# Splitting the modulation products of a two-layer diffusion backbone over two column groups of TensorE, with one buffer for each row made during routing

## The chip, the cores and the metric

The kernel runs on one core of a Trainium2 chip. The metric is the device time of one execution in microseconds (us); a lower time is better. TensorE (PE in the profile) does the matrix products, VectorE (DVE) and ScalarE (ACT) the elementwise work, GpSimd (POOL) and SyncE (SP) issue the DMAs here. "Record" below means one matmul instruction as the trace lists it; an f32 product of 128 rows by 512 columns appears as two records.

## What is computed

A backbone of two layers over 256 latent tokens and 256 context tokens, model width 1024. Cut to what matters:

```python
for l in range(DEPTH):                                   # DEPTH = 2
    mod   = silu(c)     @ w_mod[l] + b_mod[l]            # (1, 6144), for latent tokens
    mod_c = silu(c_ctx) @ w_mod[l] + b_mod[l]            # (6144,),  for context tokens
    sh1, sc1, g1, sh2, sc2, g2 = split(mod, 6)           # and the same of mod_c
    h = rmsnorm(x, norm1[l]) * (1 + sc1) + sh1
    q, k, v of three branches, gates = split(h @ w_in[l])
    x = x + g1 * merge(global attention, window attention, neighbourhood attention)
    h = rmsnorm(x, norm2[l]) * (1 + sc2) + sh2
    x = x + g2 * moe(h)        # 16 experts of width 512, top 2 inside the best group of 4
return rmsnorm(x, final_norm)
```

The context tokens go through layer 0 in the same way and serve as keys and values in both. The modulation vectors are two rows (one for `c`, one for `c_ctx`) of 6144 values per layer. All products are f32.

## The kernel before

**Weights.** All weights but the small ones pass through a ring of six SBUF slots of 2 MB (`ring`, `WR[slot]`). SyncE issues the loads in one fixed order (`plan_units`, `load`, L422 for `w_mod` and `w_in`, L438 for experts). A load into a slot waits until the last product that read the slot is done (`releases`); the first twelve loads also keep three in flight (`AHEAD = 3`: load i waits for modulation i-3).

**Modulation.** The 6144 columns of a layer are made in twelve pieces of 512, numbered i = 0 to 23 over both layers, j = 0 to 11 within one. `modulation(i)` on TensorE (L1369) multiplies `cT` (128 x 2 per step) by the 2 MB slot in KD = 8 steps, 16 records, into rows 0 and 1 of one PSUM bank, `MOD_BANK[i]`; a bank that was used before is waited for by `mod_row`. `mod_rows(i)` on VectorE adds the bias (L920; L916 and L917 for the two scale parts, which are also multiplied with the norm weight) and writes a row buffer `mrow` of 2 x 512. `store_mod` on GpSimd (L518) stores the buffer to DRAM (`mod_d`), from where GpSimd later loads it back broadcast over 128 partitions (`load_modb` L528, `load_gout` L549).

**When they run.** Twelve pieces of layer 0 come first. Between them stand the four transposes of the first normed rows (`transpose_h`, L1348), and behind them the projections of layer 0 (L1418), of which the first needs the `kvab` weights. Of layer 1, piece 12 comes right behind the router product (L1502), before TensorE waits for VectorE's selection (`sel_ready`) and computes positions (L1535, L1538); pieces 13 to 19 follow it and then the first expert's transposes (`transpose_rows(0)`). Pieces 20 to 23 follow the last expert of layer 0.

**Routing.** VectorE computes for every token its two experts and slots, with `mod_rows(12)` in the middle and `mod_rows(13..19)` behind. As soon as the slots are known (`slot_ready`), GpSimd scatters the 512 normed tokens twice to DRAM (`hs_d`, eight indirect DMAs, L591), waits for all of them, loads the rows of experts 0 and 1 (`load_rows`, L600), and only then stores the modulation rows 13 to 19 one after the other, loads the modulation of layer 1 (L528) and the rows of expert 2.

**Row buffers.** In layer 0 four buffers rotate, in layer 1 two: before it writes row i, VectorE waits for the store of row i-4, or i-2 in layer 1 (`mod_store`).

**Experts.** Three 2 MB weights per expert (gate L1584, up L1591, down L1614). An expert with at most 64 rows takes another form, two products in the upper and lower 64 output partitions at the same time (gate and up L1598, down L1620).

## Time and profile before

| | |
|---|---|
| median of 3 runs | 1875.71 us (1874.19 to 1879.04) |
| the profiled execution | 1875.32 us |
| its span | 1873.7 us |
| TensorE busy | 1696.4 us, 91% |
| VectorE busy | 463.4 us, 25% |
| ScalarE busy | 339.6 us, 18% |
| moved by DMA | 396.74 MB, mean 212 GB/s |
| matmuls of the modulation, L1369 | 384 records, 170.6 us |

The page divides the span into 40 slices of 46.8 us and gives each engine's busy share in tenths. The timeline gives merged runs of equal instructions in order of time: start, length, engine, line, operation, count, and in brackets the idle time before and what ended it. The stretches view gives busy time, granted TensorE clock (1.00 is 2.4 GHz, 0.50 is 1.2 GHz), DMA share and GB/s of a stretch; a DMA share of about 1.04 is the highest that lasts.

### The profile page before, as it was taken

What the parts mean: (1) busy time and instruction counts of PE and PEld (TensorE: products, weight loads), DVE (VectorE), ACT (ScalarE), POOL (GpSimd) and SP (SyncE); (2) the same over time, 40 slices, a digit from 0 to 9 for tenths busy, and PEclk for the clock granted to TensorE, in tenths of its full rate; (3) what the DMA queues carried; (4) which work ended last, traced back from release to release, by engine and by line L of the source; (5) the groups of instructions that cost most, each with busy time, mean ns of one, the idle gap of its engine ahead of it and who ended that gap; (6) DMA issues with size and microseconds to landing.
All of it is one profiled execution on the core that took longest, in us unless ns stands there. A gap on an engine that the chain in (4) does not pass through costs nothing. (4 is left out here: it accounts for less than half of the span.)

```text
span 1873.7 us, 15998 instructions
## 1 busy us (share of the span) xinstructions
PE 1696.4 (91%) x6163; PEld 758.0 (40%) x6163; DVE 463.4 (25%) x1206; ACT 339.6 (18%) x759; POOL 132.2 (7%) x219
## 2 busy tenths in 40 slices
PE   7999998889999999999999989998799949987871
PEld 1244445554444445244444324445544424432220
DVE  0324016760011123210110145207601140011003
ACT  1011117770000012010010012017600111010001
POOL 0110000010000000210000020000200010001001
PEclk9999999999999998999999999999999969998886
DMA  9971323012213044899999997243234177999992
GB/s 337 369 250 51 90 96 141 14 28 68 78 57 134 0 147 146 332 372 357 391 387 393 395 382 232 91 113 146 55 117 155 45 279 271 323 370 385 380 393 99
DMA packets 178194, 396.74 MB, mean 212 GB/s; under 512 B 23694, under 2 KB 27822, under 8 KB 177928
## 3 DMA queue, kind: packets, MB, share of 16 engines
q1 hardware_dynamic: 160256, 327.17, 49.0%
q0 software_dynamic: 17136, 66.13, 9.5%
q10 hardware_dynamic: 724, 2.38, 0.3%
q8 instruction: 51, 0.84, 0.2%
q14 instruction: 27, 0.22, 0.0%
HBM read 373.27 MB, written 34.18 MB: 217 GB/s over the span
## 5 line engine op out<-in xcount | busy, mean ns | idle before, releaser
L1418 PE MATMUL bank<-ring_sb,HT_sb 128*128 128x512 f32 x672 | 297.0, 597 | 2.7 <-ACT HT_sb L701 1.5
L1483 PE MATMUL bank<-ring_sb,HT_sb 128*128 128x512 f32 x576 | 253.3, 592 | 1.4 <-ACT QR_sb L792 1.4
L1598 PE MATMUL bank<-ring_sb,QR_sb 128*64 128x512 f32 x608 | 149.7, 649 | 42.0 <-DMA ring_sb<-w_e_up 42.0
L1418 PEld LDWEIGHTS bank<-ring_sb,HT_sb 128*128 128x128 f32 x672 | 126.2, 192 | 150.2 <-issue 148.3
L1369 PE MATMUL bank<-ring_sb,cT_sb 128*2 128x512 f32 x384 | 170.6, 605 | 1.6 <-DMA ring_sb<-w_mod 1.6
L1483 PEld LDWEIGHTS bank<-ring_sb,HT_sb 128*128 128x128 f32 x576 | 109.3, 190 | 138.7 <-issue 136.8
L1487 PE MATMUL bank<-ring_sb,QR_sb 128*128 128x512 f32 x288 | 129.5, 592 | 0.0
L1598 PEld LDWEIGHTS bank<-ring_sb,QR_sb 128*64 128x64 f32 x608 | 49.8, 149 | 128.0 <-issue 127.9
L1459 PE MATMUL bank<-WK_sb,KR_sb 128*64 128x128 f32 x960 | 68.3, 280 | 36.3 <-ACT WK_sb L802 35.5
L1584 PE MATMUL bank<-ring_sb,QR_sb 128*128 128x512 f32 x208 | 94.2, 606 | 3.4 <-ACT QR_sb L838 3.4
L1614 PE MATMUL bank<-ring_sb,QR_sb 128*128 128x512 f32 x208 | 91.8, 594 | 0.0
L1591 PE MATMUL bank<-ring_sb,QR_sb 128*128 128x512 f32 x208 | 91.4, 592 | 0.0
L1369 PEld LDWEIGHTS bank<-ring_sb,cT_sb 128*2 128x2 f32 x384 | 32.4, 86 | 134.7 <-issue 131.7
L1459 PEld LDWEIGHTS bank<-WK_sb,KR_sb 128*64 128x64 f32 x960 | 50.9, 136 | 81.0 <-ACT WK_sb L802 81.0
L811 ACT ACTIVATE WK_sb<-bank 128x512 f32<-128x512 f32 x36 | 21.5, 597 | 341.7 <-PE bank L1483 341.7
L1513 PE MATMUL bank<-ring_sb,HT_sb 128*128 128x512 f32 x192 | 83.1, 592 | 0.0
L1487 PEld LDWEIGHTS bank<-ring_sb,QR_sb 128*128 128x128 f32 x288 | 54.7, 190 | 68.9 <-issue 68.9
L1442 PE MATMUL bank<-KR_sb,QR_sb 64*128 64x512 f32 (+1 forms) x288 | 70.5, 568 | 4.5 <-ACT MB_sb L785 2.9
L1620 PE MATMUL bank<-ring_sb,QR_sb 128*64 128x512 f32 x304 | 69.4, 598 | 1.4 <-DVE QR_sb L1256 0.8
L1101 DVE TENSOR_TENSOR WK_sb<-WK_sb,bank 128x512 f32<-128x512 f32 x24 | 16.5, 689 | 214.7 <-PE bank L1487 214.7
L802 ACT ACTIVATE WK_sb<-bank 128x512 f32<-128x512 f32 (+1 forms) x144 | 67.3, 521 | 10.8 <-PE bank L1470 10.7
L1470 PE MATMUL bank<-tab_sb,MB_sb 128*128 128x128 f32 x480 | 68.2, 281 | 0.0
(209 smaller groups left out, 1333.1 us busy)
## 6 DMA issues: line engine op xcount, KB each, us to landing
ring_sb<-w_e_gate SPq DMA_DIRECT2D x32, 2048.0 KB, 18.7
ring_sb<-w_e_up SPq DMA_DIRECT2D x32, 2048.0 KB, 21.0
ring_sb<-w_e_down SPq DMA_DIRECT2D x32, 2048.0 KB, 20.4
ring_sb<-w_mod SPq DMA_DIRECT2D x24, 2048.0 KB, 12.5
ring_sb<-w_in SPq DMA_DIRECT2D x22, 2048.0 KB, 15.7
MB_sb<-mod_d POOLq DMA_DIRECT2D x16, 512.0 KB, 8.2
ring_sb<-w_branch SPq DMA_DIRECT2D x8, 1024.0 KB, 10.1
ring_sb<-w_out SPq DMA_DIRECT2D x4, 2048.0 KB, 10.3
```

What stands on the lines that cost most here:

```text
L1369: ins = mm(bank[use][0:2, :], cT[:, k, :], WR[slot][:, k], start=(k == 0), stop=(k == KD - 1))
L1418: ins = mm(bank[j % 4][:, :], HT[:, k, P * t:P * t + P], WR[slot][:, k], start=(k == 0), stop=(k == KD - 1))
L1442: mm(sbank[(2 * p + side) % 4][:, w], qT[b][part, j, P * t:P * t + P], kT[b][part, j if b == N else 0, w], start=True, stop=True).then_inc ...
L1459: ins = mm(dst, v, PT[side][:, k], start=(k == ks[0]), stop=(k == NT - 1))
L1483: ins = mm(bank[i % 2][:, :], HT[:, k, P * t:P * t + P], WR[wg][:, k], start=(k == 0), stop=(k == KD - 1))
L1487: ins = mm(bank[2 + i % 2][:, :], qT[n][:, k, P * t:P * t + P], wdown[wb][:, k, CW * half:CW * half + CW], start=(k == 0), stop=(k == 3))
L1513: ins = mm(bank[i % 3][:, :], HT[:, k, P * t:P * t + P], WR[slot][:, k], start=(k == 0), stop=(k == KD - 1))
L1584: ins = mm(bank[0][:, :], hgT[q % 2][:, k], WR[gate][:, k], start=(k == 0), stop=(k == KD - 1))
L1591: ins = mm(bank[1][:, :], hgT[q % 2][:, k], WR[up][:, k], start=(k == 0), stop=(k == KD - 1))
L1598: ins = mm(bank[0][HALF * side:HALF * side + HALF, :], hgT[q % 2][:, k, 0:HALF], WR[slot][:, k], start=(k == 0), stop=(k == KD - 1))
L1614: ins = mm(bank[4 + half][:, :], eaT[:, k], wdown[slot][:, k, CW * half:CW * half + CW], start=(k == 0), stop=(k == 3))
L1620: ins = mm(bank[4][HALF * half:HALF * half + HALF, :], eaT[:, k, 0:HALF], wdown[slot][:, k, CW * half:CW * half + CW], start=(k == 0), sto ...
```

## The change

Each modulation product is split in two: steps 0 to 3 of the contraction go to output rows 0 and 1 of the bank (column group 0), steps 4 to 7 to rows 64 and 65 (column group 64), issued in turns. `mod_mm` now counts two per piece. VectorE adds the bias to the second half and then adds the first half, so that each row takes one VectorE instruction more. The eight rows of layer 1 that are made during routing get a buffer each, in `HT` (free at that time), so that VectorE waits for no store there; GpSimd waits for all stores up to row 19 before it loads the modulation of layer 1.

```diff
+        mrow1 = [HT[0:2, j, :] for j in range(MOD_GAP)] + [mrow[j % 2] for j in range(MOD_GAP, NMOD)]
...
             if key[0] == "mod":
-                return mod_mm, NMOD * key[1] + key[2] + 1
+                return mod_mm, 2 * (NMOD * key[1] + key[2] + 1)
...
                     if l == 0 and AHEAD <= i < NMOD:
-                        eng.wait_ge(mod_mm, i - AHEAD + 1)
+                        eng.wait_ge(mod_mm, 2 * (i - AHEAD + 1))
...
-                dma(mod_d[l, :, CW * j:CW * j + CW], mrow[i % (2 if l else 4)]).then_inc(mod_store[i % 4], 16)
+                dma(mod_d[l, :, CW * j:CW * j + CW], mrow1[j] if l else mrow[j % 4]).then_inc(mod_store[i % 4], 16)
...
                     load_bmod(1, WK[0:2, 0:2 * D], MOD_GAP)
+                    mod_stored(NMOD + MOD_GAP)
                     load_modb(1, 0)
...
-                eng.wait_ge(mod_mm, i + 1)
-                n = 2 if l else 4
-                if i >= n:
-                    eng.wait_ge(mod_store[(i - n) % 4], 16 * ((i - n) // 4 + 1))
-                row, b, made = mrow[i % n], bmod[i], bank[MOD_BANK[i]][0:2, :]
+                eng.wait_ge(mod_mm, 2 * (i + 1))
+                last_use = i - 4 if l == 0 else i - 2 if j >= MOD_GAP + 2 else -1
+                if last_use >= 0:
+                    eng.wait_ge(mod_store[last_use % 4], 16 * (last_use // 4 + 1))
+                row, b = mrow1[j] if l else mrow[j % 4], bmod[i]
+                made = [bank[MOD_BANK[i]][HALF * side:HALF * side + 2, :] for side in range(2)]
                 part, half = divmod(j, 2)
+                link(tt(row, made[1], b, ALU.add))
                 if part in (1, 4):
-                    link(tt(row, made, b, ALU.add))
+                    link(tt(row, row, made[0], ALU.add))
...
                 else:
-                    tt(row, made, b, ALU.add).then_inc(mod_row, 1)
+                    tt(row, row, made[0], ALU.add).then_inc(mod_row, 1)
...
-                for k in range(KD):
-                    ins = mm(bank[use][0:2, :], cT[:, k, :], WR[slot][:, k], start=(k == 0), stop=(k == KD - 1))
-                ins.then_inc(mod_mm, 1)
+                for k in range(KD // 2):
+                    for side in range(2):
+                        ins = mm(bank[use][HALF * side:HALF * side + 2, :], cT[:, KD // 2 * side + k, :],
+                                 WR[slot][:, KD // 2 * side + k], start=(k == 0), stop=(k == KD // 2 - 1))
+                        if k == KD // 2 - 1:
+                            ins.then_inc(mod_mm, 1)
```

## Rows read from the trace of the kernel before

**Rows 1.** Page, slices of 46.8 us: TensorE and the DMA share.

```profile
PE   7999998889999999999999989998799949987871
DMA  9971323012213044899999997243234177999992
```

**Rows 2.** Timeline of TensorE, layer 0's pieces and the first projections.

```profile
78.46 7.03 PE L1369 MATMUL bank<-ring_sb,cT_sb 128*2 128x512 f32 x16
...
102.31 20.77 PE L1418 MATMUL bank<-ring_sb,HT_sb 128*128 128x512 f32 x48
```

**Rows 3.** Timeline of TensorE, an expert in either form, and a short gap.

```profile
864.08 7.09 PE L1598 MATMUL bank<-ring_sb,QR_sb 128*64 128x512 f32 x32
...
879.38 7.13 PE L1584 MATMUL bank<-ring_sb,QR_sb 128*128 128x512 f32 x16
...
1036.13 7.09 PE L1598 MATMUL bank<-ring_sb,QR_sb 128*64 128x512 f32 x32 [1.77 <-DMA ring_sb<-w_e_up]
```

**Rows 4.** Waits of SyncE's queue, 0 to 130: total us, times, longest.

```profile
SPq L422 <- PE bank L1369: 66.3, 11, 10.6
```

**Rows 5.** DMA issues: count, KB each, median us to landing.

```profile
X_sb<-x ACTq DMA_DIRECT2D x2, 512.0 KB, 7.9
...
tab_sb<-tab ACTq DMA_DIRECT2D x1, 272.5 KB, 8.1
```

**Rows 6.** Stretches: PE, PEld, DVE, ACT, POOL busy, clock, DMA share, GB/s.

```profile
0.00:10.00 10.00, 0.04 (x1) 0.07 (x2) 0.00 (x0) 1.28 (x1) 1.90 (x7) 1.00 0.68 241
10.00:20.00 10.00, 9.30 (x21) 2.23 (x22) 0.00 (x0) 0.18 (x1) 0.00 (x0) 1.00 0.92 341
...
90.00:100.00 10.00, 10.00 (x30) 2.47 (x28) 0.68 (x1) 1.09 (x2) 0.52 (x1) 1.00 1.06 385
```

**Rows 7.** Timeline of TensorE, routing of layer 0.

```profile
744.61 8.63 PE L1369 MATMUL bank<-ring_sb,cT_sb 128*2 128x512 f32 x16
...
801.77 1.09 PE L1348 MATMUL bank<-tab_sb,QR_sb 128*128 128x128 f32 x8
804.04 7.13 PE L1584 MATMUL bank<-ring_sb,QR_sb 128*128 128x512 f32 x16 [1.18 <-ACT QR_sb L838]
```

**Rows 8.** Timeline of VectorE and GpSimd, routing of layer 0.

```profile
753.34 0.68 DVE L920 TENSOR_TENSOR KR_sb<-bank,QR_sb 2x512 f32<-2x512 f32 x1 [2.25 <-PE bank L1369]
...
791.13 0.68 DVE L916 TENSOR_TENSOR KR_sb<-bank,QR_sb 2x512 f32<-2x512 f32 x1 [22.19 <-DMA mod_d<-KR_sb]
...
759.92 1.04 POOL L591 DMA_INDIRECT hs_d<-QR_sb,slot_i_sb  x1 [5.10 <-DVE slot_i_sb L1209]
...
782.14 1.14 POOL L600 DMA_DIRECT2D QR_sb<-hs_d  x2 [12.29 <-DMA hs_d<-QR_sb,slot_i_sb]
...
809.15 0.53 POOL L600 DMA_DIRECT2D QR_sb<-hs_d  x1
```

**Rows 9.** Timeline of TensorE in layer 1's experts: a product behind a longer gap.

```profile
1712.81 8.78 PE L1598 MATMUL bank<-ring_sb,QR_sb 128*64 128x512 f32 x32 [3.66 <-DMA ring_sb<-w_e_up]
```

**Rows 10.** The two row loads issued at 782: time to landing.

```profile
DMA to landing us min/median/max: 6.6/7.3/8.1
```

**Rows 11.** Timeline of TensorE, routing of layer 1, where no pieces run.

```profile
1546.66 1.97 PE L1348 MATMUL bank<-tab_sb,QR_sb 128*128 128x128 f32 x8 [18.58 <-DMA QR_sb<-hs_d]
1549.81 8.91 PE L1584 MATMUL bank<-ring_sb,QR_sb 128*128 128x512 f32 x16 [1.18 <-ACT QR_sb L838]
```

**Rows 12.** Stretches of 5 us, columns as in rows 6.

```profile
745.00:750.00 5.00, 5.00 (x9) 0.81 (x8) 4.30 (x22) 0.00 (x0) 0.00 (x0) 0.71 0.45 169
750.00:755.00 5.00, 5.00 (x26) 1.27 (x25) 2.55 (x11) 0.00 (x0) 0.52 (x1) 1.00 0.13 16
...
875.00:880.00 5.00, 5.00 (x16) 2.22 (x15) 1.12 (x2) 0.60 (x1) 0.00 (x0) 1.00 0.97 325
```

**Rows 13.** Timeline at the end of layer 0: TensorE, then VectorE.

```profile
1121.24 1.94 PE L1348 MATMUL bank<-tab_sb,WK_sb 128*128 128x128 f32 x8 [3.90 <-DVE WK_sb L940]
...
1112.42 0.68 DVE L916 TENSOR_TENSOR KR_sb<-bank,WK_sb 2x512 f32<-2x512 f32 x1
```

## The prediction

> **What bounds the kernel now.** I read the page's slices first: TensorE is at 9 nearly everywhere, so time is saved where TensorE's own work is on the path, unless something else is right behind it. The DMA row shows where that may be: it is at 9 in the first slices and from slice 17 on, the experts of layer 0 [rows 1]. The modulation runs in three places, and each has another neighbour, so I take them one by one: pieces 0 to 11 at the start, 12 to 19 in the routing of layer 0, 20 to 23 at its end.
>
> **What a piece costs.** Now 16 records, one behind the other, take 7.03 us [rows 2]. For two column groups the expert of at most 64 rows is the nearest row: 32 records in 7.09 us, against 16 in 7.13 for a full expert [rows 3]. The two groups fully overlap there, 0.22 us a record against 0.44. A modulation product differs in having 2 columns for 64. I take 3.5 us per piece, half of now. Bounds: 3.5 by that row, 7.0 if nothing overlaps.
>
> The Trainium skill, "TensorE: Matmul & The Clock Gate", section on packing small matmuls, says that a weight load overlaps a running matmul only when the row groups differ. Here both groups use all 128 rows, so by that rule some or all of the gain could be missing. The 0.22 us of rows 3 is the same situation and speaks against it; the rule stays as a rival below.
>
> **Start, pieces 0 to 11.** TensorE is the bound: SyncE waits 66.3 us in 11 waits for its products before it issues the next load [rows 4], and the first projection starts at 102.31 [rows 2]. But the DMA is nearly full too. With pieces at 3.5 us it becomes the bound. How far that reaches is a sum of bytes. Ahead of the first projection must land twelve pieces and the `kvab` weights, 13 x 2.097 = 27.26 MB, four tiles of X of 0.52 MB and four broadcasts of the modulation of the same size, 4.19 MB, and the table, 0.28 [rows 5]: 31.7 MB. By 20 us, 2.41 + 3.41 = 5.82 MB have moved. The rest at the full stretch's 0.385 MB/us takes 67.3 us: 87.3 [rows 6]. The last piece lands 5.4 us before, its product ends near 85.5 and the last transpose (1.1 us) [rows 7] near 86.6, so `kvab` is last. Loads stay queued: load i is issued when piece i-3 is done, 3.5 us after landing, with 10.8 us of loads behind it. **Gain 102.3 - 87.3 = 15.0 us.** The projections behind it take about 28 us per 2 MB unit of weights, so the DMA gets ahead again and the gain stays. VectorE gets one more instruction of 0.68 us [rows 8] per row; the longest row with its normed tile is then some 4.9 us, inside the 5.4 us per load: cost 0. If that cover went, the excess would be 0.1 to 1 us a piece.
>
> **TensorE's clock there.** The gaps are 5.4 - 3.5 = 1.9 us. Behind a gap of 1.77 us the product ran at full speed, 7.09 [rows 3]; behind one of 3.66 it took 8.78, the granted clock having been at its lower level, 1.2 GHz, for part of it [rows 9]. 1.9 is next to the first, so I take 0; the other bound is 1.7 us once at the end of the stage, as the gaps before do not count while the DMA is the bound.
>
> **Routing, pieces 12 to 19.** TensorE runs from 744.61 to 801.77 through the eight pieces and then starts expert 0 [rows 7]. After the change, piece 12 ends near 749.8 (it starts at the lower clock, as now). The selection comes at 751.1 as now, the positions take 0.5, and seven pieces end at 751.7 + 7 x 3.5 = 776, or some us later by waits for banks. What is late next is the rows of expert 0. GpSimd starts the scatters at 759.92, all have landed at 782.14, and the two row loads issued there land in 6.6 and 8.1 us [rows 8, 10]. VectorE's row 12 moves: now it runs at 753.34 behind piece 12, and afterwards at 751.1, with two instructions till 752.5, so that the slots come 1.4 us earlier. The scatters move 4.2 MB in 22.2 us, 0.19 MB/us: half of the DMA, the other half being weight loads, which are always queued in that stretch already. So I keep their length: landed at 780.8, rows at 788.5. TensorE then restarts 13.3 us earlier than now, after a gap of 12 us. In layer 1, where the same place has no pieces, it restarts behind 18.58 us with 1.97 for the transposes and 8.91 for the first gate, against 1.09 and 7.13 [rows 7, 11]: 2.7 us given back. TensorE's side moves by 10.6.
>
> The buffers matter here. Today VectorE's row 15 waits 22.19 us for a store that GpSimd can issue only behind the scatters [rows 8]; this costs nothing now, since the bank it holds is wanted later. With pieces of 3.5 us, piece 19 would wait for row 16, made near 792. With own buffers rows 13 to 16 follow at 1.4 to 2.1 us each from 761.3, and banks come free in time to about 1 us.
>
> **What the DMA lets through.** Behind the routing it is full to the end of layer 0's experts (slices 17 to 23) [rows 1], and there TensorE stalls a little on weights (1.77 us) [rows 3]. The gain that survives is the DMA's idle time that vanishes. With 1.05 as full, the idle of the 27 stretches of 5 us from 745 to 880 adds up to 13.4 us; rows 12 show the first (2.9), the largest (4.4) and the last (0.4). By place it is 7.3 from 745 to 755, 1.7 from 760 to 770, 1.5 from 805 to 820 and 3.0 from 860 to 880 [rows 12]. Piece 12 frees its slot 3.4 us earlier, piece 13 closes the gap at 760 (1.6), experts that start earlier close 1.5 at 805 and up to 3.0 at 860: 9.5 at most, 6.5 without the last. **I take 9.0**; bounds 4 (the scatters are pushed back by the earlier loads) and 10.6.
>
> **The added wait of GpSimd** for the stores up to row 19: the stores are issued from about 783 to 787 and land some 6 to 12 us later, near 795. Behind it are queued the modulation loads and the rows of expert 2, now issued at 809.15 [rows 8]. TensorE wants those two experts (some 33 us) after 788.5. Cost 0, with over 10 us of slack.
>
> **End of layer 0, pieces 20 to 23.** TensorE waits 3.90 us for VectorE behind them [rows 13], so their saving of up to 14 us is worth nothing. VectorE's chain (gathered rows, sum, norm) is the path, and row 21 stands in it at 1112.42: one instruction more, 0.7 us **lost**. Rows 22 and 23 come behind the first normed tile, and the later tiles have 3 us of slack. Cost 0.7, bound 2.1 (all three rows).
>
> **The sum.** 1875.3 (the profiled execution, 0.4 under the median of three) - 15.0 - 9.0 + 0.7 = 1852.0; against the median 1852.4.
>
> **The rivals.**
> (A) *The routing gain is eaten by the DMA*: the weight loads issued 9 to 22 us earlier take bandwidth from the scatters, and the rows come hardly earlier than now. The first scatter landed when no load competed, which speaks for it; that all later ones already shared, against. With a gain of 0 to 4 there: 1857 to 1861.
> The Trainium skill, "DMA: Bandwidth & Descriptors", section on queues and rings, says that each DMA engine takes turns between the queue rows it has work for, packet by packet. By that, more loads in SyncE's one row do not shrink GpSimd's half; the 0.19 MB/us agrees, and rival A would need the opposite.
> (B) *The column groups do not overlap*: pieces stay at 7.0 us, TensorE keeps both stretches, VectorE's 0.7 is added: 1876.0, no change. The rule on weight loads above would give this. The two forms of an expert speak against [rows 3].
> (C) *Slower: TensorE's clock falls in the gaps of the start.* At 1.2 GHz a piece in two groups takes twice 3.5 = 7.0 us, as long as now. If each gap of 1.9 us sufficed, the twelve pieces would take 84 us, the seven of routing 49, nothing would be won, and the first projection and expert 0 would each pay the 2.7 us of a start at that level: with the 0.7, 1875.3 + 6.1 = 1881.4. What decides is whether the gaps of 1.9 us go with the row of 1.77 or with that of 3.66 [rows 3, 9]. Against it: the longer pieces would themselves close the gaps.
> (D) *More*: the scatters also gain, the DMA catches up, TensorE's 10.6 is kept in full and a little more: 1847 to 1850.
>
> **How the numbers follow.** The forecast, 1850 to 1857, 0.64; A 0.19; B 0.05; C 0.03; D 0.09. A measurement tells a change from none at about 0.3%, 5.6 us. Faster: 0.64 + 0.19 + 0.09 = 0.92, less 0.01 for A's far end; same 0.06; slower 0.03. The range for 8 in 10 takes the forecast, D down to 1848 and A up to 1860.
>
> **What would show it.** L1369: 16 records in 3.5 us. First projection near 87, and before it a wait for `ring_sb<-w_in`. At routing: TensorE idle some 12 us until the rows of expert 0, at about 788 less 15, and a granted clock below 1.00 right behind. Layer 0's last expert earlier by 24. In front of layer 1's first transposes a longer wait for VectorE, not an earlier start of that chain. I am wrong if the projection waits for something else than the DMA, if the scatters land later than 22 us behind their start, or if the DMA idles again between 750 and 880.

## The result

Measured: **1853.07 us** (median of 4 runs, 1849.80 to 1855.26) against 1874.95 us for the kernel before on the same chip (4 runs, 1873.92 to 1879.04). The ratio is 0.9877, with a 95% interval of 0.9857 to 0.9896. The profiled execution took 1853.53 us, its span was 1851.9. Now and then an execution falls into a slower state with a lower granted clock (2091.69 us once in the kernel before, 1903.82 once in an experiment); such runs are left out of every median here.

| | before | after |
|---|---|---|
| span of the profiled execution | 1873.7 us | 1851.9 us |
| TensorE busy | 1696.4 us, 91% | 1625.3 us, 88% |
| VectorE busy | 463.4 us, 25% | 481.4 us, 26% |
| matmuls of the modulation (384 records) | 170.6 us | 95.9 us |

On TensorE 75 us of modulation time have gone, but only 22 us of the run. The rows below tell where the other 53 went. The lines have moved by a few: the modulation's matmul is now L1374, the transposes L1352, the projections L1425, the router L1509, the scatters L592, the row loads L601; a row is now made by L918 and L924, or for the scale parts by L918, L920 and L921.

**Start.** Timeline of TensorE in the changed kernel (start, length, engine, line, operation, count, and in brackets the idle time before it and what ended it):

```profile
21.95 5.30 PE L1374 MATMUL bank<-ring_sb,cT_sb 128*2 128x512 f32 x16 [4.93 <-DMA ring_sb<-w_mod]
28.49 3.60 PE L1374 MATMUL bank<-ring_sb,cT_sb 128*2 128x512 f32 x16 [1.25 <-DMA ring_sb<-w_mod]
33.93 3.60 PE L1374 MATMUL bank<-ring_sb,cT_sb 128*2 128x512 f32 x16 [1.84 <-DMA ring_sb<-w_mod]
39.45 3.60 PE L1374 MATMUL bank<-ring_sb,cT_sb 128*2 128x512 f32 x16 [1.91 <-DMA ring_sb<-w_mod]
46.29 5.16 PE L1374 MATMUL bank<-ring_sb,cT_sb 128*2 128x512 f32 x16 [3.24 <-DMA ring_sb<-w_mod]
...
87.52 1.09 PE L1352 MATMUL bank<-tab_sb,WK_sb 128*128 128x128 f32 x8
89.98 20.87 PE L1425 MATMUL bank<-ring_sb,HT_sb 128*128 128x512 f32 x48 [1.37 <-DMA ring_sb<-w_in]
```

A piece takes 3.60 us, against 7.03 in [rows 2], and TensorE now waits for the weights ahead of nearly every piece. The first projection starts at 89.98, 12.3 us earlier than in [rows 2]. The stretches of the same kernel (columns as in rows 6) show a DMA that stays full from 20 us on. The kernel before had it full from 20 to 40 too, but then at shares of 0.98 and 0.90 (351 and 321 GB/s) from 40 to 60, and at 370 and 373 GB/s from 70 to 90:

```profile
20.00:30.00 10.00, 6.81 (x24) 1.22 (x26) 1.36 (x2) 5.36 (x11) 0.52 (x1) 0.83 1.05 392
...
50.00:60.00 10.00, 5.05 (x24) 0.82 (x20) 3.54 (x6) 0.00 (x0) 1.04 (x2) 0.99 1.04 398
...
80.00:90.00 10.00, 7.81 (x43) 2.64 (x39) 4.37 (x6) 2.17 (x4) 1.17 (x3) 1.00 1.08 363
```

**Routing.** TensorE of the changed kernel, from the last transposes ahead of the router to expert 0:

```profile
717.78 1.04 PE L1352 MATMUL bank<-tab_sb,QR_sb 128*128 128x128 f32 x8
718.65 7.31 PE L1509 MATMUL bank<-wr_sb,HT_sb 128*128 128x16 f32 x48
...
732.45 5.12 PE L1374 MATMUL bank<-ring_sb,cT_sb 128*2 128x512 f32 x16
...
739.42 10.47 PE L1374 MATMUL bank<-ring_sb,cT_sb 128*2 128x512 f32 x48
750.68 13.90 PE L1374 MATMUL bank<-ring_sb,cT_sb 128*2 128x512 f32 x64 [0.80 <-DVE HT_sb L924]
777.39 1.97 PE L1352 MATMUL bank<-tab_sb,QR_sb 128*128 128x128 f32 x8 [12.81 <-DMA QR_sb<-hs_d]
780.53 10.20 PE L1591 MATMUL bank<-ring_sb,QR_sb 128*128 128x512 f32 x16 [1.18 <-ACT QR_sb L840]
```

Pieces 13 to 19 run through with one stall of 0.80 us, and TensorE is idle for 12.81 us until expert 0's rows are there. TensorE then restarts slowly: 10.20 us for the first gate against 7.13 in [rows 7]. In the stretches view the granted clock there is 0.50, which is 1.2 GHz (columns as in rows 6):

```profile
775.00:780.00 5.00, 1.97 (x8) 1.57 (x8) 0.00 (x0) 0.60 (x2) 0.73 (x2) 0.50 1.04 392
```

GpSimd's timeline shows what it waited for:

```profile
746.26 1.04 POOL L592 DMA_INDIRECT hs_d<-QR_sb,slot_i_sb  x1 [5.10 <-DVE slot_i_sb L1213]
...
770.09 1.14 POOL L601 DMA_DIRECT2D QR_sb<-hs_d  x2 [13.92 <-DMA hs_d<-QR_sb,slot_i_sb]
771.23 2.02 POOL L519 DMA_DIRECT2D mod_d<-HT_sb  x4
...
781.70 2.12 POOL L529 DMA_DIRECT2D MB_sb<-mod_d  x4 [5.97 <-DMA mod_d<-HT_sb]
783.82 0.53 POOL L601 DMA_DIRECT2D QR_sb<-hs_d  x1
```

The scatters take 23.8 us from the first issue to the last landing, 22.2 in [rows 8]. The added wait lasts 5.97 us and costs nothing: the rows of expert 2 behind it are issued at 783.82, against 809.15 in [rows 8]; about 12 of these 25 us come from the start.

**End of layer 0.** TensorE, the first of pieces 20 to 23 and the first work of layer 1:

```profile
1068.56 3.60 PE L1374 MATMUL bank<-ring_sb,cT_sb 128*2 128x512 f32 x16
...
1100.80 1.94 PE L1352 MATMUL bank<-tab_sb,WK_sb 128*128 128x128 f32 x8 [9.03 <-DVE WK_sb L944]
```

Piece 20 starts where the experts end, 21.15 us earlier than before (1089.71). Layer 1's first transposes start 20.4 us earlier than in [rows 13], behind a wait for VectorE of 9.03 us where it was 3.90. So most of what the four pieces save there (5 us more of wait for VectorE, and new waits for weights between the pieces) is idle time now, and 0.7 us are lost.

### The profile page after: what moved, and what is told of

Its sections match the earlier page's. It is cut to its first block and busy times, and to the rows that moved or that the text cites. A ratio compares the mean times of both kernels' runs of the same rounds, so it can differ in the third digit from the quotient of the medians.

```text
span 1851.9 us, 16016 instructions
## 1 busy us (share of the span) xinstructions
PE 1625.3 (88%) x6163; PEld 743.8 (40%) x6163; DVE 481.4 (26%) x1230; ACT 339.5 (18%) x759; POOL 131.6 (7%) x219
## 5 line engine op out<-in xcount | busy, mean ns | idle before, releaser
L1425 PE MATMUL bank<-ring_sb,HT_sb 128*128 128x512 f32 x672 | 296.0, 596 | 4.1 <-ACT HT_sb L703 1.5
L1425 PEld LDWEIGHTS bank<-ring_sb,HT_sb 128*128 128x128 f32 x672 | 125.8, 191 | 151.2 <-issue 147.6
L1494 PE MATMUL bank<-ring_sb,QR_sb 128*128 128x512 f32 x288 | 129.5, 592 | 0.0
L1374 PE MATMUL bank<-ring_sb,cT_sb 128*2 128x512 f32 x384 | 95.9, 651 | 31.1 <-DMA ring_sb<-w_mod 30.3
L1591 PE MATMUL bank<-ring_sb,QR_sb 128*128 128x512 f32 x208 | 98.4, 629 | 3.4 <-ACT QR_sb L840 3.4
L1621 PE MATMUL bank<-ring_sb,QR_sb 128*128 128x512 f32 x208 | 91.8, 594 | 0.0
L1598 PE MATMUL bank<-ring_sb,QR_sb 128*128 128x512 f32 x208 | 91.4, 592 | 0.0
L1245 DVE TENSOR_TENSOR QR_sb<-QR_sb,bank 128x512 f32<-128x512 f32 x13 | 8.9, 688 | 211.0 <-PE bank L1598 211.0
```

The costliest lines, as they stand in the source:

```text
L1374: ins = mm(bank[use][HALF * side:HALF * side + 2, :], cT[:, KD // 2 * side + k, :], WR[slot][:, KD // 2 * side + k], start=(k == 0), stop= ...
L1425: ins = mm(bank[j % 4][:, :], HT[:, k, P * t:P * t + P], WR[slot][:, k], start=(k == 0), stop=(k == KD - 1))
L1494: ins = mm(bank[2 + i % 2][:, :], qT[n][:, k, P * t:P * t + P], wdown[wb][:, k, CW * half:CW * half + CW], start=(k == 0), stop=(k == 3))
L1591: ins = mm(bank[0][:, :], hgT[q % 2][:, k], WR[gate][:, k], start=(k == 0), stop=(k == KD - 1))
L1598: ins = mm(bank[1][:, :], hgT[q % 2][:, k], WR[up][:, k], start=(k == 0), stop=(k == KD - 1))
L1621: ins = mm(bank[4 + half][:, :], eaT[:, k], wdown[slot][:, k, CW * half:CW * half + CW], start=(k == 0), stop=(k == 3))
```

## The experiments

The table reads the timelines of the runs in one way: from the last transposes ahead of layer 0's router (717.78 in the row above), so that what happened at the start drops out. All columns are in us. "Router" is the length of the router's first 48 records. "Scatters" is their start, "length" the time from there until the rows' load is issued, and `up` the start of expert 0's second product. "Experts' end" is the start of piece 20, right behind layer 0's experts; the column after it is the same less the router's length, which no edit touched and which varies. "To layer 1" is the time from the experts' end to layer 1's first transposes.

| kernel | router | scatters | length | up | experts' end | less router | to layer 1 |
|---|---|---|---|---|---|---|---|
| before | 7.23 | 29.90 | 22.2 | 80.99 | 359.69 | 352.46 | 31.5 |
| buffers only | 6.03 | 29.97 | 22.2 | 81.05 | 359.35 | 353.32 | 31.6 |
| split, two rotating buffers | 6.17 | 27.36 | 21.6 | 76.90 | 355.28 | 349.11 | 32.4 |
| split at the start only | 5.43 | 28.31 | 22.3 | 79.38 | 358.36 | 352.93 | 31.4 |
| split in routing only | 5.43 | 26.12 | 22.9 | 68.71 | 347.30 | 341.87 | 31.4 |
| after | 7.31 | 28.48 | 23.8 | 72.79 | 350.78 | 343.47 | 32.2 |
| after, again | 7.95 | 29.12 | 22.8 | 70.22 | 350.67 | 342.72 | 31.8 |
| after, beside the last one | 7.47 | 28.64 | 23.7 | 72.69 | 350.85 | 343.38 | 32.2 |
| sides in turn | 6.91 | 28.91 | 23.2 | 70.91 | 349.33 | 342.42 | 32.2 |
| fillers in layer 0 | 6.12 | 27.30 | 23.0 | 66.24 | 347.70 | 341.58 | 32.9 |
| rows first | 5.44 | 26.60 | 23.0 | 69.13 | 347.72 | 342.28 | 32.3 |
| row 21 early | 6.20 | 27.37 | 23.6 | 70.73 | 349.02 | 342.82 | 30.3 |
| `kvab` in long rows | 6.66 | 27.84 | 23.3 | 70.55 | 349.49 | 342.83 | 32.3 |
| row 21 and fillers | 5.52 | 26.68 | 24.7 | 69.31 | 347.42 | 341.90 | 30.8 |

**The buffers alone.** The kernel before, with the eight buffers and GpSimd's wait, no split:

```diff
+        mrow1 = [HT[0:2, j, :] for j in range(MOD_GAP)] + [mrow[j % 2] for j in range(MOD_GAP, NMOD)]
...
+                    mod_stored(NMOD + MOD_GAP)
```

> The kernel before with the eight row buffers and GpSimd's added wait, but with no piece split. Main theory: VectorE's wait of 22.19 us for a store goes, nothing on the path does, since the eight pieces keep TensorE busy until 801.8: 1875, within 2 us of before, expert 0's transposes at 801.8. Rival (the buffers alone bring part of the gain of 9 us in the routing): 1866 to 1872.

1874.54 us against 1875.54, ratio 1.0000 (0.9986 to 1.0013). The buffers by themselves are worth nothing, as forecast: VectorE's wait of 22.19 us [rows 8] is gone in this kernel, and nothing on the path moved with it (expert 0's transposes at 801.92 for 801.77).

**The split without the buffers.**

```diff
-        mrow1 = [HT[0:2, j, :] for j in range(MOD_GAP)] + [mrow[j % 2] for j in range(MOD_GAP, NMOD)]
+        mrow1 = [mrow[j % 2] for j in range(NMOD)]
...
-                last_use = i - 4 if l == 0 else i - 2 if j >= MOD_GAP + 2 else -1
+                last_use = i - 4 if l == 0 else i - 2
```

> The changed kernel with two rotating buffers for all rows of layer 1, as before the change. Main theory: VectorE's row 15 waits for the store of row 13, which GpSimd issues only behind the scatters (771.2 in the changed kernel) and which lands some 6 us later, row 16 follows near 780.5 and frees the bank of piece 19, so that this piece ends near 784.5 and expert 0's transposes start there instead of at 777.4: 5 to 7 us slower than the changed kernel at that point, 1858 to 1860 in all. Rival (the buffers cover nothing, as the rows of expert 0 land later than all that): 1853.

1862.19 us, ratio 0.9931 (0.9914 to 0.9949): 9 us slower than with the buffers, and 2 us more than forecast. TensorE of this kernel:

```profile
780.14 6.20 PE L1374 MATMUL bank<-ring_sb,cT_sb 128*2 128x512 f32 x16 [19.28 <-DVE KR_sb L924]
786.27 1.09 PE L1352 MATMUL bank<-tab_sb,QR_sb 128*128 128x128 f32 x8
788.53 7.13 PE L1591 MATMUL bank<-ring_sb,QR_sb 128*128 128x512 f32 x16 [1.18 <-ACT QR_sb L840]
```

Piece 19 waits 19.28 us for a bank whose row VectorE could not write (VectorE itself waits 24.08 us for a store), takes 6.20 us behind that gap, and expert 0 stands behind it. Expert 0's transposes start 8.9 us later than in the changed kernel (786.27 for 777.39), but its second product only 4.9 (795.51 for 790.57), because piece 19 pays for the slow restart in expert 0's stead. At layer 1's first transposes the kernel is 5.5 us late (1106.28 for 1100.80), inside the 5 to 7 that were forecast; the other 3 us arise in layer 1's experts, which this edit does not touch, and there profiles of unaltered kernels differ as much (see "A spread" below). So 5.5 us of the 9 are shown to come from the buffers.

**The split at one place at a time.** `split(i)` chooses per piece (its first form is the kernel with the start only, its second the one with the routing only); elsewhere the 16 records run in one column group, as before.

```diff
+def split(i):
+    return i < NMOD
...
+    return NMOD <= i < NMOD + MOD_GAP
...
+                if not split(i):
+                    for k in range(KD):
+                        ins = mm(bank[use][0:2, :], cT[:, k, :], WR[slot][:, k], start=(k == 0), stop=(k == KD - 1))
```

> The changed kernel, but only pieces 0 to 11 (layer 0) split; buffers kept. Main theory: the gain of the start alone, 12.3 us by the trace of the changed kernel, remains to the end: 1862.5, first projection at 90. VectorE's end of layer 0 as before. Rival (the later DMA-bound experts take the gain of the start back): 1870 or more.

> The changed kernel, but only pieces 12 to 19 split; buffers kept. Main theory: the gain of the routing alone, 9.0 us by the traces at the end of layer 0's experts: 1866, first projection at 102.3, the interval from the router product to expert 0's transposes 45 us instead of 57. Rival (the two gains depend on each other through the DMA): a sum of the two gains that differs from 21 us by more than 3.

Start only: 1864.01 us, ratio 0.9940 (0.9922 to 0.9957), so 11.5 us; its first projection starts at 90.36. Routing only: 1865.42, ratio 0.9953 (0.9935 to 0.9971), so 10.1 us. Together they give 21.6, against the whole 21.9. Each of these gains is uncertain by about 3 us, and within that the two places are independent. The start gave less than its 15.0, which the timeline confirms (about 12); that the routing gave more than its 9.0 is not shown. In both, the way from the experts' end to layer 1 is 31.4 us and not 32.2, as pieces 20 to 23 are not split: the 0.7 us of the third place, seen alone.

**The sides one behind the other.** The records of a piece in another order: all of column group 0, then all of group 64.

```diff
-                for k in range(KD // 2):
-                    for side in range(2):
+                for side in range(2):
+                    for k in range(KD // 2):
```

> The changed kernel with the same sixteen records per piece in another order: first the four steps of one column group, then the four of the other. Main theory: records overlap only when neighbours in the queue are in different column groups, so that this order takes 6.9 us per piece, as in the kernel before, plus VectorE's 0.7 us at the end of layer 0: 1876. Rival (any split of the work by column groups is as good, or the shorter sums bring the gain): 3.5 us per piece, 1853.

1858.00 us, ratio 0.9904 (0.9888 to 0.9921). This expectation of 1876 was a clear miss: most of the gain stays. TensorE and its weight loads (PEld) in this kernel:

```profile
74.25 5.32 PE L1374 MATMUL bank<-ring_sb,cT_sb 128*2 128x512 f32 x16
...
742.20 27.10 PE L1374 MATMUL bank<-ring_sb,cT_sb 128*2 128x512 f32 x112
...
75.54 0.09 PEld L1374 LDWEIGHTS bank<-ring_sb,cT_sb 128*2 128x2 f32 x1 [0.34 <-issue]
75.97 0.09 PEld L1374 LDWEIGHTS bank<-ring_sb,cT_sb 128*2 128x2 f32 x3 [0.34 <-issue]
76.40 0.09 PEld L1374 LDWEIGHTS bank<-ring_sb,cT_sb 128*2 128x2 f32 x2 [0.34 <-issue]
```

A piece alone takes 5.32 us, and seven in a row 27.10: with 5.32 for the first, 3.63 for each of the others ((27.10 - 5.32) / 6). So records of one column group run beside those of the other although the program puts up to eight of a kind in a row. The weight loads fit that: every 0.43 us one load starts (two at 74.25), and from 75.97 to 76.83 two or three. A likely reading is that TensorE takes records of the idle group ahead of queued ones of the busy group, over some records and across the border of two pieces, but not over a whole piece at once. The trace does not name a record's group, so this reading is argued and not shown, and how far TensorE would look ahead was not measured. Alternating the sides, as the changed kernel does, is worth 1.7 us for a piece that stands alone and next to nothing in a row of pieces.

**Products that nobody reads, in the gap.** 13 constant products stand between piece 19 and expert 0's transposes, in layer 0:

```diff
+                if l == 0:
+                    for k in range(13):
+                        mm(bank[2][:, :], ident, tab[:, 0:CW], start=True, stop=True)
                 transpose_rows(0)
```

> The changed kernel with 13 products of a constant table (11.3 us at full clock, their output is not used) on TensorE between piece 19 and expert 0's transposes, where it is idle for 12.8 us; only layer 0. They end before the rows land. Theory P (TensorE's own side bounds the experts of layer 0 at their start): the granted clock stays at 1.00, the transposes take 1.1 for 2.0 and the first gate product 7.1 for 10.2, and the end of layer 0's experts comes 4.0 us earlier: 1849. Theory D (the DMA is the bound, as the prediction had it): the start of the second expert moves by 4 us, but stalls for weights come back and the end of the experts moves by 1 us at most: 1852 to 1853.

```profile
763.39 11.43 PE L1641 MATMUL bank<-tab_sb 128*128 128x512 f32 x26
774.83 1.10 PE L1352 MATMUL bank<-tab_sb,QR_sb 128*128 128x128 f32 x8
777.10 7.13 PE L1591 MATMUL bank<-ring_sb,QR_sb 128*128 128x512 f32 x16 [1.18 <-ACT QR_sb L840]
```

The restart is at full speed: 1.10 and 7.13 us where the changed kernel had 1.97 and 10.20. Yet the time is 1853.58 us, ratio 0.9874 (0.9858 to 0.9891), no change. In the table `up` starts at 66.24, the earliest of all and 6.55 us ahead of the changed kernel; 1.2 of these are a shorter router. At the experts' end, less the router, 1.9 us are left of the other 5.4 (341.58 for 343.47), about where three kernels with a later `up` also end (341.87 to 342.28). The stretches from 840 to 855, first of the changed kernel:

```profile
840.00:845.00 5.00, 5.00 (x20) 2.15 (x20) 1.26 (x2) 0.60 (x1) 0.51 (x1) 1.00 0.85 297
845.00:850.00 5.00, 5.00 (x26) 1.71 (x24) 0.00 (x0) 0.00 (x0) 0.55 (x2) 1.00 0.96 330
850.00:855.00 5.00, 5.00 (x20) 2.46 (x17) 0.68 (x1) 1.68 (x3) 0.00 (x0) 1.00 0.94 341
```

and then with the fillers:

```profile
840.00:845.00 5.00, 5.00 (x28) 2.00 (x25) 0.12 (x1) 0.60 (x1) 0.00 (x0) 1.00 1.06 386
845.00:850.00 5.00, 5.00 (x15) 2.37 (x14) 1.26 (x2) 1.08 (x2) 0.00 (x0) 1.00 1.02 363
850.00:855.00 5.00, 5.00 (x15) 2.14 (x15) 0.42 (x1) 0.60 (x1) 1.10 (x2) 1.00 1.04 391
```

In this profile of the changed kernel the DMA still idled there (shares 0.85 to 0.96), so TensorE set the pace; with the fillers it is full. The two later profiles of the changed kernel show both cases: 0.88 to 0.96 in the one, 1.03 to 1.05 in the other, whose first gate took only 8.67 us. Less the router, the kernels that are not split in routing end at 352.46 to 353.32, the changed kernel at 342.72 to 343.47, and the fillers, the routing-only kernel, the rows-first kernel and the combination at 341.58 to 342.28. So the DMA lets through some 11 us (10.2 to 11.7), and the changed kernel stands 0.4 to 1.9 us above that floor. Theory D had at most 1 us at the experts' end and is right in the main; whether the last 1.9 us reach the end can't be read from the total, since layer 1's experts alone differ by more.

**Do the weight loads slow the scatters?** Expert 1's gate and all loads behind it wait until the scatters have landed:

```diff
+                    if l == 0 and (q, j) == (1, 0):
+                        eng.wait_ge(rows_put, 32 * NT)
                     load_expert(l, q, q, j)
```

> The changed kernel, but SyncE issues the weights of expert 1 and the down weights of expert 0 only when all scattered rows have landed (layer 0 only). Theory A (weight loads in flight take bandwidth from the scatters, in proportion to their number): the scatters land 4 to 8 us earlier than at 23.8 us behind their start, and TensorE starts expert 0 by as much earlier. Theory S (the DMA shares equally between the two queues as long as one load is waiting; three are still ahead): the scatters land within 2 us of where they do now, and the later issue of three loads costs nothing or a few us at expert 1: 1853 to 1857.

1851.70 us (three runs, 1851.00 to 1857.71), ratio 0.9880 (0.9857 to 0.9904). The scatters take 23.0 us with the loads held back. Without that they took 22.8 to 24.7 in nine profiles with the pieces of routing split and buffered. So how many loads are queued behind does not set their length, and holding these back wins nothing that shows. Rival A, a routing gain of 0 to 4 us, falls by the measured gain of 9 to 10. The run does not show what the scatters would take with no load beside them: two 2 MB loads were issued in that time instead of four, and the DMA share stayed at 1.00 to 1.05. In layer 1 of the changed kernel the four scatters of half as many rows take 8.9 us (1512.36 to 1521.23), less than half of 23.8, while the DMA share falls from 1.02 to 0.48. That loads in flight slow the scatters thus stays possible.

**Row 21 ahead of the gathered rows.** On VectorE at the end of layer 0:

```diff
-                        if t < 2:
-                            mod_rows(NMOD + MOD_GAP + t)
+                        if t == 0:
+                            mod_rows(NMOD + MOD_GAP)
+                            mod_rows(NMOD + MOD_GAP + 1)
```

> The changed kernel with VectorE's row 21 made before the first gathered rows instead of between the first and the second tile. Main theory: the three instructions of row 21 (2.1 us) leave the chain that ends layer 0, and layer 1's first transposes come 2.1 us earlier: 1851. Rival (another wait takes its place: the gathers or the clock): no change at the transposes.

```profile
1097.03 1.94 PE L1353 MATMUL bank<-tab_sb,WK_sb 128*128 128x128 f32 x8 [7.03 <-DVE WK_sb L944]
```

The wait is 7.03 us, 2.0 less than in the changed kernel; the way to layer 1 is 30.3 us for 32.2. That settles that row 21's three instructions stood in VectorE's chain. The total, 1853.59 us (0.9880, 0.9863 to 0.9896), does not resolve 2 us.

**The `kvab` weights in long rows.** The first weights behind the pieces are read in pieces of 1 KB; here as rows of 2 KB. That takes other columns of `w_in`, so this kernel leaves out the right keys and values; the bytes and the work are the same. It ran once.

```diff
-                    return [(slice(256 * i, 256 * i + 256), w[:, KV_COL[i]:KV_COL[i] + 256]) for i in range(2)]
+                    return [(slice(0, CW), w[:, 0:CW])]
```

> The changed kernel, but the kvab weights are read as 512 neighbouring columns (rows of 2 KB) instead of two blocks of 256 columns (pieces of 1 KB). These are other columns of w_in than the ones meant, so this part of the computation is changed; the bytes and the work are the same. What is asked is why the first projection started at 90.0 and not at 87.3. Theory P: the stretch from 80 to 90 us, in which kvab arrives, moves 363 GB/s where the full stretches before move 387, because of its small pieces; with 2 KB rows it moves 385 or more and the first projection starts at about 89.4 (0.6 us earlier; at most 1 us). Theory T: the lower rate has another reason (the requests of other queues that fall into this stretch), the stretch stays near 363 and the start at 90.0 to 90.4. In both the rest, some 2 us, is in about 1 MB more that has moved by then than I had summed.

```profile
80.00:90.00 10.00, 8.44 (x45) 3.01 (x42) 4.61 (x6) 2.17 (x4) 1.02 (x3) 1.00 1.05 386
...
89.60 20.87 PE L1425 MATMUL bank<-ring_sb,HT_sb 128*128 128x512 f32 x48 [0.75 <-DMA ring_sb<-w_in]
```

386 GB/s in the stretch that had 363, and the projection starts at 89.60, against 89.98, 90.06 and 90.39 in three profiles of the changed kernel. The small pieces cost 0.4 to 0.8 us, by this one profile.

**A combination, beside the changed kernel.** Row 21 early, the fillers also in layer 1's routing (16) and 4 ahead of layer 1's first transposes. The changed kernel ran twice more, the second time on the chip of the combination.

```diff
+                for k in range(16 if l else 13):
+                    mm(bank[2][:, :], ident, tab[:, 0:CW], start=True, stop=True)
...
+                    for k in range(4):
+                        mm(bank[6][:, :], ident, tab[:, 0:CW], start=True, stop=True)
```

> The changed kernel once more, unaltered, on the chip and beside the runs of the combination below, since its differences are near the spread between chips. Both theories: ratio to the kernel before 0.988 within 0.002; first projection at about 90, last expert of layer 0 done about 21 us earlier than in the kernel before.

> The changed kernel, unaltered, on the chip and beside the runs of the combination below. Both theories: ratio to the kernel before 0.988 within 0.002.

> The changed kernel with three additions: row 21 ahead of the gathered rows on VectorE; constant f32 products that nobody reads in the idle stretches of TensorE, so that it restarts at the granted clock 1.00: 13 in the routing gap of layer 0, 16 in that of layer 1 (where TensorE idles 18.3 us), and 4 behind piece 23, ahead of layer 1's first transposes. Nothing of the computation is left out. Theory K (what is saved behind the last wait of a stage is kept unless the DMA is full behind it): row 21 gives 2.0 us; the start of layer 1 gives up to 2.5 (first projection 7.1 us for 8.9 to 9.7, transposes 1.1 for 1.9); layer 0's routing gives 0 to 1, since the DMA is full behind it; layer 1's routing gives the full 2.7 (8.8 to 7.1, 1.97 to 1.1) if the DMA idles somewhere behind it and 0 if it is full. Sum against the unaltered changed kernel on the same chip: 4 to 8 us faster. Theory N (the low clock at a restart costs only where the records show it, but every stage behind it hides it): only the 2.0 of row 21 are seen in the time, 0 to 2.5 us in all.

The changed kernel: 1854.42 us (0.9878, 0.9861 to 0.9894), and 1856.03 (0.9897, 0.9881 to 0.9914). The combination, on the chip of the latter: 1852.30 us (1848.63 to 1853.14), 0.9877 (0.9861 to 0.9894). All four runs of the combination (the slowest 1853.14) are below all four of the changed kernel there (the fastest 1855.65), the medians differ by 3.7 us and the profiled spans by 7.2 (1846.9 and 1854.1). The 3.7 lie between theory K's 4 to 8 and theory N's 2.5 at most; four runs each don't part the two. Of the 7.2 in the profiles 2.0 are a shorter router, which is chance. The rows of the combination, with its restart in layer 0 first:

```profile
776.48 1.09 PE L1353 MATMUL bank<-tab_sb,QR_sb 128*128 128x128 f32 x8 [2.01 <-DMA QR_sb<-hs_d]
778.75 8.83 PE L1592 MATMUL bank<-ring_sb,QR_sb 128*128 128x512 f32 x16 [1.18 <-ACT QR_sb L840]
...
1087.47 3.70 PE L1690 MATMUL bank<-tab_sb 128*128 128x512 f32 x8
1096.33 1.94 PE L1353 MATMUL bank<-tab_sb,WK_sb 128*128 128x128 f32 x8 [5.16 <-DVE WK_sb L944]
1099.49 8.88 PE L1426 MATMUL bank<-ring_sb,HT_sb 128*128 128x512 f32 x16 [1.22 <-issue]
...
1502.24 15.76 PE L1641 MATMUL bank<-tab_sb 128*128 128x512 f32 x32
1521.13 1.10 PE L1353 MATMUL bank<-tab_sb,QR_sb 128*128 128x128 f32 x8 [3.13 <-DMA QR_sb<-hs_d]
1523.40 8.56 PE L1592 MATMUL bank<-ring_sb,QR_sb 128*128 128x512 f32 x16 [1.17 <-ACT QR_sb L840]
```

In layer 0 the same 13 fillers that gave back the whole restart above gave back less here: the rows came 2.01 us behind the last filler, the transposes took 1.09 us, but the gate 8.83 for 7.13. The four fillers ahead of layer 1 did nothing: 5.16 us idle still followed, and transposes and projection run as slowly as before (1.94 and 8.88; 1.94 and 8.91). Those in layer 1's routing give back 0.9 us of transposes (1.10 for 1.97), and the gate takes 8.56 us where the changed kernel took 9.81 beside it; a wait of 3.13 us still stood ahead. Together they are the 2.1 us by which the distance from transposes to second product shrank (10.67 for 12.79: 1521.13 to 1531.80, 1525.27 to 1538.06). Row 21's 2.0 us are the other gain. Beside the changed kernel on the same chip this version is faster by 3.7 us; its ratio of 0.9877 is no lower than the changed kernel's first (0.9877) or the fillers' (0.9874), so it can't be called the fastest of all.

## Why the prediction was right, step by step

**The total** of 1852.4 is 0.7 us beside the measured 1853.07, and that is closer than its terms were, so part of it is luck. The start was forecast at 15.0 and measured at 12.3 in the profile and 11.5 alone. The routing was forecast at 9.0; it measured 8.9 in the profile (9.0 less the router) and 10.1 alone, where 3 us can't be told apart. The forecast span at layer 1's first transposes (15.0 + 9.0 - 0.7 = 23.3 us earlier) was missed by 2.9 (20.4), and the total came out within 0.7 us because 1.4 came back in what follows, by no edit, and 0.8 by the kernel before, whose median was 1874.95 and not 1875.71 this time. The end of layer 0 was right.

**A piece: 3.5, measured 3.60.** The neighbouring form of an expert [rows 3] gave the price well, though it has 64 columns for 2. Rival B falls. One ground of it was a rule of the Trainium skill, "TensorE: Matmul & The Clock Gate", section on packing small matmuls, that a weight load overlaps a running matmul only if the row groups differ. Here both column groups use all rows, and 16 records take 3.60 us for 7.03, so the gain that rival B had missing is there. As far as the profile shows weight loads, it too speaks against the rule for this form: in the kernel before, between 73.48 and 76.48, a load of 0.09 us starts every 0.43 us and TensorE has no idle time between the products, in one row group and one column group. The ends of products are modelled in the profile, so this is shown by the pace and not record by record.

**The start: the mechanism held, the sum of bytes was short by 2.7 us.** The DMA did become the bound, and `kvab` was last. The stretches from 0 to 90 add up to 32.8 MB (GB/s by their length: 2.42, 3.36, 3.92, 3.87, 3.87, 3.98, 3.87, 3.87 and 3.63), where I had summed 31.7. At 0.386 MB/us, the mean from 20 to 90, the missing 1.1 MB are 2.8 us. Half of it stands in the list of the DMA issues up to 92 us (count, KB each):

```profile
masks_sb<-masks POOLq DMA_DIRECT2D x1, 320.0 KB, 6.0
mod_d<-KR_sb POOLq DMA_DIRECT2D x12, 4.0 KB, 5.0
tabh_sb<-tabh POOLq DMA_DIRECT2D x1, 65.0 KB, 5.8
QR_sb<-b_mod POOLq DMA_DIRECT2D x1, 48.0 KB, 5.4
```

Those are 0.49 MB that I left out as small. The other 0.6 must be what else moved by then, the queued weights behind `kvab` above all; that is by subtraction and was not tested. The small pieces of `kvab` cost 0.4 to 0.8 us (363 for 386 GB/s), which a faster stretch, 398 from 50 to 60, made up for. So the term that was mis-sized is the start's 15.0, and the step that failed is the list of what must land, read as if nothing else moved.

**The clock in the gaps: right for this kernel, by a small margin.** Behind 1.91 us a piece took 3.60, behind 3.24 already 5.16, behind 4.93 it took 5.30. The granted clock in the stretch from 20 to 30, which holds the last of these, was 0.83 in the mean, a mixture of 2.4 and 1.2 GHz. None of it cost anything while the DMA was the bound, as forecast. Rival C falls by the rows between 28 and 45 us: three gaps of 1.25 to 1.91 us, three times 3.60. But the length of a gap does not decide alone. In ten profiles that alternate the sides at the start, every piece behind a gap up to 1.97 us took 3.60 except the kernel's first one, every piece behind 3.9 us or more took longer, and in between both occur. Row of the kernel with fillers, then a row of the combination:

```profile
39.64 5.30 PE L1374 MATMUL bank<-ring_sb,cT_sb 128*2 128x512 f32 x16 [1.98 <-DMA ring_sb<-w_mod]
...
1083.94 3.60 PE L1375 MATMUL bank<-ring_sb,cT_sb 128*2 128x512 f32 x16 [3.13 <-DMA ring_sb<-w_mod]
```

So the gaps of 1.9 us stood near the edge of what rival C needed.

**Routing: the order of things was right, three sizes were not.** TensorE did wait some 12 us (12.81) for expert 0's rows, with the granted clock at its lower level behind. (1) The restart cost 3.9 us and not 2.7: 10.20 us for the gate and not the 8.91 of layer 1 [rows 11]. That is partly chance: across the profiles of this code the gate took 8.67 to 10.20, and the changed kernel itself once paid only 2.4. (2) The scatters started 1.4 us earlier behind the router, as forecast (28.48 for 29.90), but took 1.6 us longer (23.8 for 22.2). By that the prediction's own condition for being wrong, scatters longer than 22 us, was met, though the kernel before with its 22.2 would have met it too. I can't name the cause: holding back loads that were queued behind did not shorten them below 23.0 (weight loads were in flight all the same), the lengths run from 22.8 to 24.7 among kernels that are alike there, they were 22.2 to 22.3 in the three without split pieces in routing, and 21.6 in the one where piece 19 was held up. (3) What the DMA lets through is not 9.5 but some 11 us. The experts' end moved from 359.7 to 347.3 with the split in routing only, but 1.8 of these 12.4 us are the router's; less the router it moved by 10.6, and by 10.9 with the fillers. The sum of idle DMA was also short: by the shares of the view, with 1.05 as full, the 27 stretches give 14.9 us and not 13.4. I had taken 9.5 of it as closable and the small rest as not; some of the rest closed too. In the changed kernel TensorE's side (`up` 8.2 us earlier behind the transposes) was the smaller in this profile, the DMA idled again from 840 to 855, which was the other condition for being wrong, and the end came 8.9 us earlier. In one of the two later profiles it did not idle there. So the routing term of 9.0 was met in this profile by a limit that I had not taken for one, and its size is partly luck.

The Trainium skill, "DMA: Bandwidth & Descriptors", section on queues and rings, has each engine take turns between the queue rows. By it, loads that start earlier in SyncE's row leave GpSimd's share as it is. The trace agrees in so far as the lengths with and without expert 1's loads queued are the same (23.0 us against 22.8 to 24.7); it does not explain the 1.6 us more than before.

**A spread of 1 to 4 us that no edit made.** The router's first 48 records take 5.43 to 7.95 us in these profiles, and all that follows in the routing moves with them: with the sides alternated the scatters start 21.2 us behind the router's length nearly every time. Row of the kernel with the split in routing only, to be held against 7.31 in the changed kernel:

```profile
731.21 5.43 PE L1524 MATMUL bank<-wr_sb,HT_sb 128*128 128x16 f32 x48
```

A second spread lies behind: from the first transposes of layer 1's experts to the end, the changed kernel took 326.7, 328.8 and 329.4 us in its three profiles, and all profiles 325.8 to 330.3. The cause was not looked for. That is why two profiles alone can't settle a term of 1 us here, and it is why routing only reached 12.4 us in its profile (10.6 less the router) and 10.1 in its runs.

**GpSimd's wait: right.** It lasted 5.97 us, and the rows of expert 2 were issued 25 us earlier than before. **End of layer 0: right**, 0.7 us for one instruction (31.4 to 31.6 us without it, 31.8 to 32.9 with it), and moving row 21 wins 2.0.

**Rival D** has a true core: some 11 us can be had at the experts' end where the changed kernel took 9.0 to 10.6. But nothing of what the fillers won in layer 0 shows in the total beyond the noise.

## What to carry to other kernels

A product with few output rows (2 here, up to 64 in the expert form) can be split over two column groups for half the time, at the price of one VectorE instruction. Before counting the gain, ask at each place what is second. Here it was the DMA at the start (12 us kept of the 41 that twelve pieces save), the routed rows, and the DMA right behind them, in the middle (9 to 11 of 27) and VectorE at the end (none of 14).

A buffer that costs nothing to lack can cost 5 to 9 us once the engine beside it gets faster: run such a pair as two experiments, each alone.

Where the DMA becomes the bound, list all that moves up to the point in question, not only what that point needs.

## What was not expected of the hardware

TensorE overlaps the two column groups even when the program does not alternate them: 5.32 us for a piece alone and 3.63 for each further one, against 3.60 alternated and 7.03 in one group. A gap of 3.24 us was enough for a piece at a partly lowered clock (5.16 us for 3.60), where the rows before had shown only 1.77 (full) and 3.66 (8.78 for 7.09); but so was one of 1.98 us in another kernel (5.30), while a piece behind 3.13 us took 3.60. And 13 constant products that fill the gap to its end keep the clock up (7.13 us for the first gate). With 2.01 us of idle time behind them the gate took 8.83 us, and 4 of them followed by 5.16 us of idle time gave nothing back (8.88 us for the first projection of layer 1).
